# Expert gathers and stores that skip empty places, expert weights loaded early, and two equal halves in the first projection

## The chip, the cores and the metric

The kernel runs on one core of a Trainium2 chip. The metric is the device time of one execution in microseconds (us); lower is better. The kernel before takes 3783.04 us, the median of three runs (3777.04 to 3783.94).

## What is computed

Two transformer blocks over 512 tokens (16 meta tokens stand ahead of them in the first), width 1024, all in float32. The part of the reference that matters here is the first block's mixture of experts, cut to its core:

```python
t = u.reshape(-1, D)                       # 512 tokens x 1024
g_p, g_idx = top_k(softmax(t @ wg + bg), 1)            # one of 8 groups
e_p, e_idx = top_k(softmax(e_logits_of_that_group), 2) # two of its 8 experts
gates = g_p * e_p / sum(e_p)
# every expert e, over the tokens xb that chose it:
hdn = silu(xb @ w_gate[e]) * (xb @ w_up[e])            # 1024 -> 512
ys  = hdn @ w_down[e]                                  # 512 -> 1024
out[token] += gate * ys
```

There are 64 experts, 1024 assignments (two for each token), and three weight matrices of 2 MB for each expert, 403 MB in all. The block's mixer (a gated linear attention and a latent attention behind one input projection of 528 columns) comes first; a second block follows, with a mixer of its own and a feed-forward that gathers single neurons by product keys.

## The kernel before, in words

The program is a row of blocks; at the end of each all engines meet. `setup` loads the activations, kept transposed as `core.h` (128 partitions x 8 x 528), and the first weights. Two weight buffers last through the kernel: `core.w.tiles` (four tiles of 128x8x128, 512 KB each) and `core.w.rows` (2 MB).

`first_mixer` (L672) runs `norm` (L127: squares on ACT, sums by a matmul with ones, the root, the product on DVE), then `project` (L202) of `w_in`: 12 output tiles, for each of them 8 contraction steps. Every step is a matmul of 16 columns (the meta tokens) and one of 512 (the others), `PIECES`; a float32 matmul stands in the trace as two instructions, each with its weight load. ACT copies a finished tile (L695). `by_token` (L277) forms `v` and the low-rank gate input, `gla` and `mla` follow, and `add_projection` (L704) adds `w_out` times their result to `core.h`; it is a `project` over the 512 main columns, whose SP queue fetches tile by tile as PE frees them (L220).

`first_ffn` (L1153) normalises and calls `route` (L711). There SP loads five constants (L749), PE forms the logits of 72 columns (L767) and turns the tokens to rows (L774), which SP writes to `token_rows` (L754). DVE finds the experts, the rank of every assignment within its expert, and its place: expert e owns places 64e to 64e+63, filled from 0 up; what is over 64 goes to spill blocks. POOL scatters the token number of each assignment to its place (L878) in a DRAM table that was cleared to zero, and SP reads the table back as `block_tok` (L758).

`experts` (L885) works through 32 pairs of experts. A pair's 128 places are the 128 partitions. POOL gathers the 128 token rows (L1001), an empty place taking the row of token 0. PE turns them (L919), DVE copies them (L969), and PE runs gate and up (L928) with one expert on each half of the array's columns. ACT applies silu (L956), DVE multiplies (L974), PE turns the hidden values (L937), DVE copies (L979), and PE runs down (L949). ACT copies the result (L962) and stores all 128 rows on its own DMA queue (L964). SP feeds a ring of 8 weight slots of 2 MB, six transfers to a pair, in the order gate, up, down; transfer n waits until the work that used its slot is done (L992). POOL also writes zeros to the 16 spill blocks (L1007). On PE the next pair's tokens are turned between up and the turning of the hidden values, so that ACT's and DVE's work is covered. A second block of the stage would run the spill blocks; no expert has over 64 tokens here, so its loops run nothing.

`combine` (L1108): POOL gathers the two result rows of every token in eight transfers of 128 rows (L1126), DVE weights and adds them (L1137, L1138), PE turns the sums (L1149) and DVE adds them to `core.h`. SP meanwhile loads the next mixer's first tiles and rows (L191, L198).

## Time and profile before

| what | value |
|---|---|
| runs of the kernel before | 3777.04, 3783.04, 3783.94 us |
| the profiled execution | 3787.08 us, span of its instructions 3785.2 us |
| mean granted TensorE clock | 0.87 |
| PE busy, share of the span | 2876.2 us, 76% |
| DVE busy | 1369.1 us, 36% |
| POOL busy | 662.6 us, 18% |
| ACT busy | 552.9 us, 15% |
| DMA | 1047.11 MB, mean 277 GB/s |

The page cuts the span into forty slices of 94.6 us: by them the first mixer takes slices 1 to 5, the router a part of 6 and 7, the experts 7 to 18, the second mixer 18 to 25, and the second feed-forward the rest. The share of busy time is a mean over stages with different limits, so the stages are read apart, by a table of stretches. [...] In a row of the timeline the square brackets hold the idle time before the instruction and what ended it.

### The profile page before, as it was taken

To read this page: it belongs to the slowest core of one execution; us is meant where nothing else is said; L and a number is where in the kernel's file an instruction comes from. 1 tells how busy PE (TensorE), PEld (TensorE's weight loads), DVE (VectorE), ACT (ScalarE), POOL (GpSimd) and SP (SyncE) were. 2 spreads that over 40 slices of the span, in tenths; PEclk is the share of its full clock that TensorE was granted. 3 is DMA by queue.
4 is the path that set the end of the run, shared out by engine and by line. 5 is a ranking of instruction groups with operands and counts; after the bars stand their busy time and mean duration, and the time that the engine had idled before them with its cause. 6 is when DMAs were issued, how large, how long until landed. Compare 5 with 4: busy or idle time off the path is not lost. (4 is left out here: it accounts for less than half of the span.)

```text
span 3785.2 us, 26001 instructions
## 1 busy us (share of the span) xinstructions
PE 2876.2 (76%) x9024; PEld 1313.4 (35%) x9024; DVE 1369.1 (36%) x3223; ACT 552.9 (15%) x1332; POOL 662.6 (18%) x592
## 2 busy tenths in 40 slices
PE   6956884777777777857657989888987787677767
PEld 3432542223333333323254433433443333233223
DVE  1033112000000000012192011566677667766774
ACT  1021100000000000001211010222222222222222
POOL 0000002000000000000120000244343444444433
PEclk9956586899999999978868999999998889888889
DMA  2100005999999999961001212599999999999998
GB/s 96 43 21 0 0 27 234 428 427 427 427 427 427 426 427 427 427 267 34 19 1 61 74 53 78 216 410 398 416 395 400 389 408 406 405 393 412 404 402 333
DMA packets 137673, 1047.11 MB, mean 277 GB/s; under 512 B 20929, under 2 KB 21713, under 8 KB 46929
## 3 DMA queue, kind: packets, MB, share of 16 engines
q0 software_dynamic: 81024, 562.08, 36.5%
q1 hardware_dynamic: 51920, 466.74, 30.1%
q10 hardware_dynamic: 4608, 16.78, 1.1%
q8 instruction: 65, 1.06, 0.1%
q14 instruction: 56, 0.45, 0.0%
HBM read 1020.35 MB, written 25.19 MB: 276 GB/s over the span
## 5 line engine op out<-in xcount | busy, mean ns | idle before, releaser
L1598 PE MATMUL psum<-peer_ring,peer_diag 128*128 128x512 f32 x2048 | 969.6, 632 | 289.9 <-ACT peer_diag L1639 289.6
L1524 POOL DMA_INDIRECT peer_ring<-in_peer_uv,peer_pick x512 | 569.4, 1112 | 1217.6 <-PE psum L1598 747.1
L1731 DVE CUSTOM_DVE_ANT_0 peer_ring<-peer_ring,sb_rows 128x1024 f32<-128x1024 f32 x512 | 618.4, 1224 | 372.6 <-DMA peer_ring<-in_peer_uv,peer_pick 370.8
L1598 PEld LDWEIGHTS psum<-peer_ring,peer_diag 128*128 128x128 f32 x2048 | 408.0, 203 | 843.7 <-issue 483.2
L928 PE MATMUL psum<-moe_w,moe_xT 128*64 128x512 f32 x2048 | 519.0, 664 | 169.3 <-DMA moe_w<-in_w_up 124.3
L974 DVE TENSOR_TENSOR moe_hd<-psum,moe_sg 128x512 f32<-128x512 f32 x32 | 22.1, 692 | 941.3 <-ACT moe_sg L956 941.3
L928 PEld LDWEIGHTS psum<-moe_w,moe_xT 128*64 128x64 f32 x2048 | 181.5, 153 | 505.8 <-issue 504.0
L232 PE MATMUL psum<-mix_xn,sb_tiles 128*128 128x512 f32 x640 | 280.4, 601 | 31.0 <-PEq L1198 20.1
L949 PE MATMUL psum<-moe_w,moe_hT 128*64 128x512 f32 x1024 | 230.0, 601 | 38.4 <-DVE moe_hT L979 33.6
L1001 POOL DMA_INDIRECT sb_tiles<-token_rows,ffn_block_tok x32 | 30.4, 949 | 906.2 <-PE psum L919 905.7
L232 PEld LDWEIGHTS psum<-mix_xn,sb_tiles 128*128 128x128 f32 x640 | 123.5, 193 | 188.0 <-issue 188.0
L1632 ACT ACTIVATE peer_acts<-peer_dots 128x2 f32<-128x2 f32 x256 | 52.0, 203 | 880.4 <-DVE peer_dots L1731 880.4
L1639 ACT ACTIVATE peer_diag<-sb_ident,peer_mix 128x128 f32<-128x128 f32 x512 | 173.5, 386 | 0.4 <-issue 0.2
L949 PEld LDWEIGHTS psum<-moe_w,moe_hT 128*64 128x64 f32 x1024 | 85.3, 138 | 161.1 <-issue 161.1
L1536 PE MATMUL psum<-ffn_hn,sb_tiles 128*128 128x512 f32 x256 | 115.4, 603 | 12.2 <-PEq L139 10.5
L956 ACT ACTIVATE moe_sg<-psum 128x512 f32<-128x512 f32 x32 | 19.1, 598 | 667.7 <-PE psum L928 667.7
L232 PE MATMUL psum<-mix1n_xn,sb_tiles 128*128 128x512 f32 (+1 forms) x384 | 107.1, 436 | 11.3 <-PEq L139 11.3
L878 POOL DMA_INDIRECT slot_tokens<-route_tok,ffn_slots x8 | 8.0, 994 | 597.6 <-DVEq L862 595.5
L962 ACT ACTIVATE sb_tiles<-psum 128x512 f32<-128x512 f32 x64 | 34.7, 595 | 326.9 <-PE psum L949 326.9
L232 PEld LDWEIGHTS psum<-mix1n_xn,sb_tiles 128*128 128x128 f32 x384 | 60.1, 198 | 58.4 <-issue 58.4
L1536 PEld LDWEIGHTS psum<-ffn_hn,sb_tiles 128*128 128x128 f32 x256 | 49.1, 193 | 74.9 <-issue 74.9
L1407 DVE TENSOR_TENSOR mix2b_z<-mix2b_z 128x2048 f32<-128x2048 f32 x1 | 2.3, 2293 | 197.3 <-PEq L214 197.3
(343 smaller groups left out, 2280.0 us busy)
## 6 DMA issues: line engine op xcount, KB each, us to landing
moe_w<-in_w_gate SPq DMA_DIRECT2D x64, 2048.0 KB, 30.2
moe_w<-in_w_up SPq DMA_DIRECT2D x64, 2048.0 KB, 33.2
moe_w<-in_w_down SPq DMA_DIRECT2D x64, 2048.0 KB, 31.0
expert_rows<-sb_tiles ACTq DMA_DIRECT2D x32, 512.0 KB, 10.2
sb_tiles<-in_w_in2b SPq DMA_DIRECT2D x28, 512.0 KB, 3.6
sb_tiles<-in_w_out SPq DMA_DIRECT2D x16, 512.0 KB, 3.5
sb_tiles<-in_w_query SPq DMA_DIRECT2D x16, 512.0 KB, 5.1
peer_ring<-in_peer_uv,peer_pick POOLq DMA_INDIRECT x512
```

Of the source, the lines that this page charges most:

```text
L232: last = nc.tensor.matmul(ps[:, u + 4 * b, 0:c.stop - c.start], wb[:, u, k], rhs[:, k, c], start=k == 0, stop=k == nk - 1)
L928: last = nc.tensor.matmul(ps[r, bank], xT[:, u, k, r], weights(slots[half], k, F, 0, F), start=k == 0, stop=k == KD - 1)
L949: last = nc.tensor.matmul(ps[r, 6 + b], hT[:, k, r], weights(slots[half], k, D, b * 512, 512), start=k == 0, stop=k == KE - 1)
L962: act.activation(yo[:, u, b * 512:(b + 1) * 512], ps[:, 6 + b], ACT.Copy).then_inc(yo_ready, 1)
L974: dve.tensor_tensor(hd[:], ps[:, 3], sg[:], ALU.mult).then_inc(hd_ready, 1)
L1001: pool.indirect_dma_start(out=xg[:, q % 2], out_offset=None, in_=T_rows, in_offset=bass.IndirectOffsetOnAxis(ap=block_tok[:, q:q + 1], axis=0)
L1524: pool.indirect_dma_start(out=ring[:, slot], out_offset=None, in_=A["peer_uv"], in_offset=bass.IndirectOffsetOnAxis(ap=pick[:, i, j:j + 1] ...
L1536: last = nc.tensor.matmul(ps[:, 4 + s], core.w.tiles[:, m % U, k], hn[:, k], start=k == 0, stop=k == KD - 1)
L1598: last = nc.tensor.matmul(ps[:, 2 * i + c], diag[:, b % DIAGS, x], ring[:, slot, D + 512 * c:D + 512 * (c + 1)], start=False, stop=end, sk ...
L1632: act.activation(acts[:, b % DIAGS], dots[:, i, j:j + BATCH], ACT.Gelu).then_inc(gelued, 1)
L1639: act.activation(diag[:, b % DIAGS, x], ident[:], ACT.Copy, scale=mix[:, b % DIAGS, x:x + 1]).then_inc(diagonal, 1)
L1731: dve.tensor_tensor_reduce(ring[:, n % RING, 0:D], ring[:, n % RING, 0:D], hr[:, i], 1.0, 0.0, ALU.mult, ALU.add, dots[:, i, j + x:j + x + ...
```

## The change

- Each place of the table now holds two numbers, the token (for the gather) and the row of the assignment, token + 512j for choice j (for the store). The table is cleared to 2048 instead of 0. Gathers and stores of the experts are both indirect transfers on POOL with a bound (511, 1023), and a place whose number is over it is to be skipped. So results lie in DRAM by assignment; `combine` reads them with four plain transfers of 1 MB on SP ahead of the next mixer's weights. The zero stores of the spill blocks are gone, and DVE clears the two gather buffers at the start.
- The store of a pair moves from ACT's queue to POOL's, behind a wait for both halves of the result; POOL issues gather q+2, then store q.
- The 8 slots of the ring, and the router's constants, are allocated outside the router and filled by SP at the end of the output projection's queue (`then`). To make room, the norm, the router and the experts place their working tiles in `core.w.rows`, `core.w.tiles` and the mixer's `y`. The experts' SP loop starts at transfer 8.
- The first mixer's norm, input projection and low-rank input take their 528 columns as 264 + 264 in place of 16 + 512.

```diff
+HALVES = (slice(0, L // 2), slice(L // 2, L))
...
+MOE_RING = 8
 MOE_BLOCKS = N_EXPERTS + SPILL + 1
+EMPTY = 4 * SEQ
...
-        sq = st.sb("sq", [P, nk, width])
-        mean = st.sb("mean", [P, width])
-        inv = st.sb("inv", [P, width])
-        rs = st.sb("rs", [P, width])
+        if room is None:
+            sq = st.sb("sq", [P, nk, width])
+            mean, inv, rs = (st.sb(n, [P, width]) for n in ("mean", "inv", "rs"))
+        else:
+            sq, (mean, inv, rs) = room
...
+                if then is not None:
+                    then(sp)
...
-            norm(core, "n1", core.h, xn, core.vec[:, VEC["mix"]], D, PIECES)
-            project(core, "in1", A["w_in"], xn, 12, PIECES,
+            norm(core, "n1", core.h, xn, core.vec[:, VEC["mix"]], D, HALVES)
+            project(core, "in1", A["w_in"], xn, 12, HALVES,
                     lambda act, m, acc, c: act.activation(zT[:, m, c], acc, ACT.Copy), following=A["w_out"])
             by_token(core, "in1v", A["w_v"], xn, v,
                      [(i, META + P * i, P) for i in range(NT)] + [(NT, 0, META)],
-                     (A["w_alow"], a_low, PIECES), gla_ahead)
+                     (A["w_alow"], a_low, HALVES), gla_ahead)
...
-                for dst, src in ((wr, "w_router"), (bias, "b_router"), (tri, "before"), (io, "iota"), (tok, "tokens")):
-                    sp.dma_start(dst[:], A[src]).then_inc(loaded, 16)
                 sp.wait_ge(own, 1)
-                sp.dma_start(slot_tok.rearrange("(p n) o -> p (n o)", p=P), zero[:]).then_inc(zeroed, 16)
+                sp.dma_start(slot_tok.rearrange("(p n) o -> p (n o)", p=P), empty[:]).then_inc(zeroed, 16)
...
-                sp.dma_start(block_tok[:], slot_tok.rearrange("(b s) o -> s (b o)", s=2 * SLOTS),
+                sp.dma_start(block_tok[:], slot_tok.rearrange("(b s) o -> s b o", s=2 * SLOTS),
...
-                            in_=tok[:, i:i + 1], in_offset=None).then_inc(scattered[j * NT + i], 16)
+                            in_=tok[:, j, i], in_offset=None).then_inc(scattered[j * NT + i], 16)
...
+        xT = work[:, 0:4].rearrange("p (u a) (k s) -> p u (a k) s", u=2, s=S2)
+        sg, hd = work[:, 4], work[:, 5]
...
-        def result_out(act, row, u, n, wait):
+            act.activation(sg, ps[:, 2], ACT.Silu).then_inc(sg_ready, 1)
+
+        def result_out(act, u, n, wait):
             act.wait_ge(used[DOWN], n + 1)
             act.wait_ge(stored[u], wait)
             for b in range(2):
                 act.activation(yo[:, u, b * 512:(b + 1) * 512], ps[:, 6 + b], ACT.Copy).then_inc(yo_ready, 1)
-            act.wait_ge(yo_ready, 2 * n + 2)
-            act.dma_start(Y_rows[row], yo[:, u]).then_inc(stored[u], 16)
...
-                for n in range(uses):
-                    if n >= RING:
-                        sp.wait_ge(used[(n - RING) % 6 // 2], (n - RING) // 6 + 1)
+                for n in range(RING, uses):
+                    sp.wait_ge(used[(n - RING) % 6 // 2], (n - RING) // 6 + 1)
                     sp.dma_start(wr[:, n % RING], source[n % 6 // 2][2 * (n // 6) + n % 2]).then_inc(landed[n % RING], 16)
 
             @block.gpsimd
             def _(pool):
-                pool.memset(zero[:], 0.0).then_inc(cleared, 1)
+                def take(q):
+                    pool.indirect_dma_start(out=xg[:, q % 2], out_offset=None, in_=T_rows,
+                                            in_offset=bass.IndirectOffsetOnAxis(ap=block_tok[:, q, 0:1], axis=0),
+                                            bounds_check=SEQ - 1, oob_is_err=False).then_inc(gathered[q % 2], 16)
+
+                for q in range(2):
+                    pool.wait_ge(cleared, q + 1)
+                    take(q)
                 for q in range(PAIRS):
-                    if q >= 2:
-                        pool.wait_ge(turned, q - 1)
-                    pool.indirect_dma_start(out=xg[:, q % 2], out_offset=None, in_=T_rows,
-                                            in_offset=bass.IndirectOffsetOnAxis(ap=block_tok[:, q:q + 1], axis=0)
-                                            ).then_inc(gathered[q % 2], 16)
-                    if q == 1:
-                        pool.wait_ge(cleared, 1)
-                        for b in range(N_EXPERTS, MOE_BLOCKS):
-                            pool.dma_start(Y_rows.rearrange("q (b s) d -> (q b) s d", s=SLOTS)[b], zero[:]).then_inc(opened, 16)
-                pool.wait_ge(opened, 16 * (SPILL + 1))
+                    if q + 2 < PAIRS:
+                        pool.wait_ge(turned, q + 1)
+                        take(q + 2)
+                    pool.wait_ge(yo_ready, 2 * q + 2)
+                    pool.indirect_dma_start(out=Y_rows, out_offset=bass.IndirectOffsetOnAxis(ap=block_tok[:, q, 1:2], axis=0),
+                                            in_=yo[:, q % 2], in_offset=None,
+                                            bounds_check=2 * SEQ - 1, oob_is_err=False).then_inc(stored[q % 2], 16)
+                for u in range(2):
+                    pool.wait_ge(stored[u], 16 * (PAIRS // 2))
...
+                    dve.memset(xg[:, u], 0.0).then_inc(cleared, 1)
...
+                placed = Y_rows.rearrange("(j i p) d -> i p j d", j=2, p=P)
+                for i in range(NT):
+                    sp.dma_start(g[:, :, i], placed[i]).then_inc(got[i], 16)
                 first_tiles(core, sp, A["w_in2a"])
                 rows_ahead(core, sp, A["w_v2"])
-
-            @block.gpsimd
-            def _(pool):
-                for i in range(NT):
-                    for j in range(2):
-                        pool.indirect_dma_start(
-                            out=g[:, j, i], out_offset=None, in_=Y_flat,
-                            in_offset=bass.IndirectOffsetOnAxis(ap=slots_u[:, j, i:i + 1], axis=0)
-                        ).then_inc(got[2 * i + j], 16)
 
             @block.vector
             def _(dve):
                 step = Chain(dve, own)
                 for i in range(NT):
-                    dve.wait_ge(got[2 * i], 16)
-                    dve.wait_ge(got[2 * i + 1], 16)
+                    dve.wait_ge(got[i], 16)
...
+                def router_then_experts(sp):
+                    for dst, src in zip(consts, ("w_router", "b_router", "before", "iota", "tokens")):
+                        sp.dma_start(dst[:], A[src]).then_inc(loaded, 16)
+                    source = expert_rows_of(A)
+                    for n in range(MOE_RING):
+                        sp.dma_start(wr[:, n], source[n % 6 // 2][2 * (n // 6) + n % 2]).then_inc(landed[n], 16)
+
+                add_projection(core, "out1", A["w_out"], y, then=router_then_experts)
+                flat = core.w.tiles[:].rearrange("p u k c -> p (u k c)")
+                norm(core, "n2", core.h[:, :, MAIN], y, core.vec[:, VEC["ffn"]], D,
+                     room=(core.w.rows, [flat[:, n * SEQ:(n + 1) * SEQ] for n in range(3)]))
+                route(core, A, y, consts, loaded, T_rows, slot_tok, slots_u, gates, block_tok, spill)
+            experts(core, A, wr, landed, y, T_rows, Y_rows, block_tok, spill)
...
+    places = np.arange(SEQ, dtype=np.uint32).reshape(NT, P).T
+    c["tokens"] = np.stack([np.stack([places, places + j * SEQ], axis=2) for j in range(2)], axis=1)
```

## Rows read from the trace of the kernel before

**Rows 1.** The page, forty slices: DMA busy tenths and GB/s.
```profile
DMA  2100005999999999961001212599999999999998
GB/s 96 43 21 0 0 27 234 428 427 427 427 427 427 426 427 427 427 267 34 19 1 61 74 53 78 216 410 398 416 395 400 389 408 406 405 393 412 404 402 333
```

**Rows 2.** Stretches: length, busy us of each engine (count), PEclk, DMA share, GB/s.
```profile
60.00:148.00 88.00, 86.95 (x321) 48.09 (x320) 0.00 (x0) 7.80 (x22) 0.00 (x0) 1.00 0.18 60
...
500.00:550.00 50.00, 40.33 (x94) 17.39 (x92) 10.50 (x12) 6.18 (x10) 0.00 (x0) 0.94 0.06 21
550.00:600.00 50.00, 24.72 (x124) 23.93 (x124) 23.41 (x99) 5.74 (x11) 2.97 (x3) 0.57 0.14 52
...
640.00:1640.00 1000.00, 779.83 (x3348) 306.70 (x3348) 75.10 (x93) 52.17 (x93) 27.40 (x29) 0.92 1.01 427
...
1645.00:1650.00 5.00, 5.00 (x22) 1.69 (x20) 0.00 (x0) 0.00 (x0) 0.00 (x0) 0.80 0.45 187
```

**Rows 3.** Waits in 610:1662: who waited for whom, us in total, times, longest.
```profile
PE psum L928 <- DMA moe_w<-in_w_up: 124.3, 32, 6.1
```

**Rows 4.** DMA issues: tensor, queue, count, KB each, median us to landing.
```profile
moe_w<-in_w_gate SPq DMA_DIRECT2D x64, 2048.0 KB, 30.2
...
expert_rows<-sb_tiles ACTq DMA_DIRECT2D x32, 512.0 KB, 10.2
...
sb_tiles<-in_w_out SPq DMA_DIRECT2D x16, 512.0 KB, 3.5
...
expert_rows<-moe_zero POOLq DMA_DIRECT2D x16, 256.0 KB, 41.3
...
sb_tiles<-token_rows,ffn_block_tok POOLq DMA_INDIRECT x32, 11.3
```

**Rows 5.** Timeline at the start of the experts: start, us, instruction [idle before it].
```profile
613.08 0.82 SPq L993 DMA_DIRECT2D moe_w<-in_w_gate  x2
...
614.18 0.99 POOL L1001 DMA_INDIRECT sb_tiles<-token_rows,ffn_block_tok  x1 [0.16 <-issue]
...
626.05 1.94 PE L919 MATMUL psum<-sb_ident,sb_tiles 128*128 128x128 f32 x8 [38.04 <-DMA sb_tiles<-token_rows,ffn_block_tok]
628.03 1.23 DVE L969 COPY moe_xT<-psum 128x1024 f32<-128x1024 f32 x1 [26.25 <-PE psum L919]
...
629.32 8.99 PE L928 MATMUL psum<-moe_w,moe_xT 128*64 128x512 f32 x32 [1.32 <-DVE moe_xT L969]
638.35 0.81 SPq L993 DMA_DIRECT2D moe_w<-in_w_up  x2
```

**Rows 6.** Timeline: last w_out tile, start of the route, its first matmul.
```profile
505.76 0.33 SPq L220 DMA_DIRECT2D sb_tiles<-in_w_out  x1
...
552.72 0.09 DVE L801 MEMSET route_zero<- 128x40 uint32 x1 [0.34 <-PEq L139]
...
556.46 13.93 PE L767 MATMUL psum<-route_wr,ffn1r_t 128*128 128x72 f32 x64 [14.29 <-DMA route_tok<-in_tokens]
```

**Rows 7.** Timeline: weight issues released by the ends of up, down, gate.
```profile
1589.87 0.80 SPq L993 DMA_DIRECT2D moe_w<-in_w_down  x2
...
1600.30 0.81 SPq L993 DMA_DIRECT2D moe_w<-in_w_gate  x2
...
1607.17 0.81 SPq L993 DMA_DIRECT2D moe_w<-in_w_up  x2
```

**Rows 8.** Timeline of combine: SP's first issue, PE's first transpose.
```profile
1673.50 1.75 SPq L191 DMA_DIRECT2D sb_tiles<-in_w_in2a  x4
...
1698.27 5.06 PEld L1149 LDWEIGHTS psum<-sb_ident,comb_g 128*128 128x128 f32 x32 [37.43 <-DVE comb_g L1138]
```

**Rows 9.** Timeline: a tile's copy in the first and in the output projection.
```profile
69.20 0.71 ACT L695 ACTIVATE mix_zT<-psum 128x16 f32 x2 [7.94 <-PE psum L232]
...
512.76 0.69 DVE L707 TENSOR_TENSOR sb_h<-sb_h,psum 128x512 f32 x1 [6.18 <-PE psum L232]
```

More of the change, by code:

```diff
@@ L8 @@
+import math
 from contextlib import ExitStack
@@ L124, in sem, with norm @@
         return self.core.sem(f"{self.name}_{name}")
-def norm(core, name, src, dst, gain, dim, pieces=(slice(0, SEQ),)):
+def norm(core, name, src, dst, gain, dim, pieces=(slice(0, SEQ),), room=None):
     nc, ps = core.nc, core.psum
@@ L199, in rows_ahead, with project @@
     core.w.loads += 1
-def project(core, name, w, rhs, n_tiles, pieces, finish, on_vector=False, following=None):
+def project(core, name, w, rhs, n_tiles, pieces, finish, on_vector=False, following=None, then=None):
     nc, ps = core.nc, core.psum
@@ L721, in route @@
     with core.stage("route") as st:
-        wr, bias = st.sb("wr", [P, KD, NR]), st.sb("bias", [P, NR])
-        tri, io, tok = st.sb("tri", [P, P]), st.sb("iota", [P, N_EXPERTS]), st.sb("tok", [P, NT], U32)
-        zero = st.sb("zero", [P, NB * SLOTS // P], U32)
-        rows = st.sb("rows", [P, NT, D])
+        wr, bias, tri, io, tok = consts
+        empty = st.sb("empty", [P, NB * SLOTS // P * 2], U32)
+        rows = core.w.rows[:].rearrange("p (i b) c -> p i (b c)", b=2)
         lg = st.sb("lg", [P, NT, NR])
@@ L800, in _ @@
                 step = Chain(dve, own)
-                step(dve.memset(zero[:], 0))
+                step(dve.memset(empty[:], EMPTY))
                 dve.wait_ge(loaded, 80)
@@ L1024, in _ @@
             def _(dve):
+                for u in range(2):
+                    dve.memset(xg[:, u], 0.0).then_inc(cleared, 1)
                 tokens_out(dve, 0, 0, 0)
@@ L1113, in combine @@
         own = st.sem("own")
-        got = [st.sem(f"got{n}") for n in range(2 * NT)]
+        got = [st.sem(f"got{n}") for n in range(NT)]
         mixed, t_ps, t_out = st.sem("mixed"), st.sem("tps"), st.sem("tout")
@@ L1158, in first_ffn @@
     with core.stage("ffn1") as st:
+        y = st.sb("y", [P, KD, SEQ])
         slots_u, gates = st.sb("slots", [P, 2, NT], U32), st.sb("gates", [P, 2, NT])
-        block_tok, spill = st.sb("block_tok", [2 * SLOTS, MOE_BLOCKS // 2], U32), st.sb("spill", [1, SPILL + 2], U32)
-        with core.stage("ffn1r") as s2:
-            t = s2.sb("t", [P, KD, SEQ])
-            norm(core, "n2", core.h[:, :, MAIN], t, core.vec[:, VEC["ffn"]], D)
-            route(core, A, t, T_rows, slot_tok, slots_u, gates, block_tok, spill)
```

117 lines of the change are left out of this document (62 added, 55 removed).

## The prediction

> **What bounds the kernel now.** I read the page's forty slices first [rows 1]: the DMA engines are full in two stretches only, slices 7 to 16 (the first block's experts) and from slice 26 on (the second block's gathers, which the change leaves alone). The table of stretches says it of the experts [rows 2]: from 640 to 1640 us the DMA share is 1.01 at 427 GB/s while PE is busy 780 of 1000 us. So there a byte costs time and an instruction does not. The waits confirm it: the up projections wait for their weights in all 32 pairs of experts, 124 us in all [rows 3]. Before the experts the DMA engines stand nearly idle: share 0.06 in 500:550 and 0.14 in 550:600 [rows 2]. [...]
>
> **What moves in the expert stage, by bytes.** 192 weight transfers of 2048 KB (2.097 MB) are 402.7 MB; 32 gathers of 128 rows of 4 KB are 16.8 MB, 32 stores of 512 KB 16.8 MB, 16 zero stores of 256 KB 4.2 MB [rows 4]. Up to the last weights (31 stores) that is 439.9 MB, at 427 GB/s 1030 us. The trace has it from the first issue at 613.1 [rows 5] to about 1647 (the share falls to 0.45 in 1645:1650 [rows 2]), 1034 us. I keep the factor 1.004 for the sum after.
>
> **Early ring.** The first 8 weight transfers and the router's 5 constants go to the SP queue behind the last tile of w_out, issued at 505.76 [rows 6]. 17 MB at 427 GB/s take 40 us, so they have landed by some 548, before the route stage begins at 552.7 and before anything else of that queue is due; only the norm computes meanwhile. Without that cover each of the 8 would cost 4.9 us. The constants are there when the router starts: its matmuls now start at 556.46, held by the last constant, and would start about 552.8: -3.7 us [rows 6]. The rest of the route (scatters of 8 bytes in place of 4, the read back of as many short runs, each now 8 bytes) is the same in count; I take 0, between 0 and +2.
>
> At the start of the experts the gather no longer queues behind weights and zeros. Before, it is issued at 614.18 and its rows are turned at 626.05, the first matmul starts at 629.32 and SP issues the next weights at 638.35 [rows 5]. Afterwards, with an empty DMA, I give the gather 3.5 us from issue to turn (a 512 KB tile lands in 3.5 [rows 4]); the memset of its buffer on DVE, which must end first, takes the place of the POOL memset ahead of it now (a copy of 128x1024 takes 1.23 [rows 5], so within 0.3 us). Turn, copy and gate projection keep their 638.35 - 626.05 = 12.3 us. So on the old time base SP issues the ninth load at 614.2 + 3.5 + 12.3 = 630.0, 16.9 us later than the first one now, but with 184 loads left.
>
> **Skipped places.** The reference's own inputs, put through its router, give 1024 assignments, 8 to 31 for each expert, so no spill block, as in the trace, and a quarter of the 4096 places filled. After the ninth load is issued there remain 184 x 2.097 = 385.9 MB of weights, and beside them 30 gathers and 31 stores. What these cost depends on how the 16 DMA engines share the rows, and the view only has their mean. An engine moves 427/16 = 26.7 GB/s, and the weights are ready when the slowest engine is. Places fill from 0 upward in each half of 64, so the filled rows sit on the low partitions of each half. Three ways:
> - Even: a quarter of the rows on each engine, 8.0 MB in all: (385.9 + 8.0)/427 x 1.004 = 926 us.
> - Half: the busiest engine holds four rows that are always filled and four that hardly ever are, where it now carries eight: 385.9/16 + 61 x 4 x 4096 B = 24.12 + 1.00 = 25.12 MB at 26.7, x 1.004 = 945 us.
> - None: an engine holds eight neighbouring places, always filled, or a skipped row moves anyway: (385.9 + 61 x 0.524)/427 x 1.004 = 983 us.
>
> Against 1034 us these give, with the start, 16.9 + 926 - 1034 = -91, -72 and -34 us. I take -72, the middle one: of the two bounds neither is nearer by any row, and the filled places being the low ones speaks against an even split. Of the -72, the early ring is 39 less the 16.9 of the later start, the zero stores 10, and the skipped places the other 40.
> [...]
>
> The stage stays bound by DMA: a pair of experts takes PE, without waits, 6.9 us for the gate (1600.30 to 1607.17, between the issues that its end and that of the work before release), as much for up, and 10.4 from there to the end of down (1589.87 to 1600.30): 24.2 us [rows 7]; DMA needs 945/30.7 = 30.8 (now 32.2). POOL has 2 indirect transfers of about 0.95 us [rows 5] in each 30.8. The store moves from ACT's queue to POOL's. POOL waits there for the pair's result; queued behind it is the gather for three pairs on, which goes out at the end of a pair and no longer after its up projection, 10.4 us later [rows 7]. PE wants it a whole pair and the next one's gate and up later, at least 30.8 + 13.8 = 44.6 us, and it lands in 11.3 [rows 4], so the wait costs nothing; with that slack gone it would cost what the landing is over it. The last store starts one POOL instruction later: +0.7 (0 to 1.5).
>
> **Combine.** Now PE starts at 1698.27, 24.8 us after SP's first issue at 1673.50 [rows 8], behind eight gathers. Afterwards four plain loads of 1 MB go first on SP: 4.2 MB at 427 GB/s are 9.8, plus 2.3 for issue and landing (a 512 KB tile moves in 1.2 and lands in 3.5 [rows 4]), plus DVE's last two passes over 128x1024, 2.4 (a copy takes 1.23 [rows 5]): 14.5. That is -10.3; I take -10 (-6 to -11). The 4 MB for the next mixer move behind them and are due only some 40 us later, after the norm.
>
> **264-column halves.** A tile of the first projection takes 7.94 + 0.71 = 8.65 us from one copy of ACT to the next; the same sixteen 512-column matmuls alone take 6.18 + 0.69 = 6.87 in the output projection [rows 9]. So sixteen 16-column matmuls cost 1.78, 0.111 each, where their columns alone would be 0.013: the weight load that each instruction has must set it. 264 columns take 6.87/16 x 264/512 = 0.221, over 0.111, so the load hides: 32 x 0.221 = 7.08 a tile, 12 x 1.57 = -18.8. The norm has sixteen such pieces more (-1.8), the low-rank extra narrow weights (-0.2). Sum -20.8. Were the load not hidden (0.33 each), it would be +22; the 512-column spacing speaks against that.
>
> **Sum.** -20.8 - 3.7 - 72 + 0.7 - 10 = -105.8. The profiled run is 3787.1 (span 3785.2), 4 over the median of 3783.0; on the median: 3677 us.
>
> **The rivals.**
> - Even split: -91 in place of -72: 3658. For it: nothing in the rows excludes it. Against: the low places.
> - No saving by skipping (or the skip is done in the engines, row by row): -34: 3715.
> - The other side: PE becomes the bound of the experts. With more of its time in work and fewer waits PE could be granted less. At clock c a pair takes 24.2/c. The rest of the change is worth 34 us, so the kernel is slower than before from (1034 - 16.9 + 34)/30.7 = 34.2 us a pair, c under 0.71. At 0.5 a pair takes 48.4 and the kernel 1486 + 16.9 - 1034 - 34 = 435 us longer: 4218. For it: 0.57 over 550:600 [rows 2]. Against: 0.92 in the experts and 1.00 where PE hardly waits [rows 2]. The low level comes after waits here, and these get shorter.
> [...]
> - The change is slight: gathers land over 44.6 us after their issue, behind the stores in POOL's queue, and cost PE the 1.4 us a pair that the bytes give: 3749, between 3740 and 3770. Against: 11.3 us now, with more bytes in flight.
>
> **How the numbers follow.** Chances: half 0.45 (3677, own range 3666 to 3692), even 0.25, none 0.18, slight 0.07, slower 0.05. The range 3648 to 3722 holds the first three but for a few per cent: about 0.83. A measurement of this kernel can tell 0.2% (7.6 us) from no change; faster 0.93, same 0.02, slower 0.05.
>
> **What would show it.** Gathers and stores with a quarter of their packets; on the new time base (24.5 us earlier by the halves and the router) the ninth weights issued near 605; the last weights landed near 1551 (even 1532, none 1589); a rate of 417 GB/s between if the busiest engine sets the pace, 425 if the split is even; router matmuls 0.2 us after the route begins; a tile of the first projection at 7.1 us. A PE without waits in the expert stage, or a granted clock under 0.8, would make the prediction wrong.

## The result, and the profile of the changed kernel

The changed kernel takes 3685.6 us (median of 4 runs, 3680.9 to 3689.3) against 3783.5: a ratio of 0.9735, interval 0.972 to 0.975. Five more runs of it in a later comparison gave 3681.6 us and 0.9725 [0.9708, 0.9742]. I compare the experiments with the middle of the two, 0.973; a thousandth of the ratio is 3.8 us, and a difference of two ratios is known to some 6 to 8 us. The forecast was 3677 us. The profiled run is 3680.9 us with a span of 3678.7, 106.5 less than before.

The page, to be read beside [rows 1]: DMA busy tenths, GB/s, and the packets with how many of them are short.

```profile
DMA  2100055999999999721002222999999999999998
GB/s 108 56 0 0 1 211 193 426 426 426 426 425 416 423 414 412 326 94 45 9 24 74 71 60 69 372 404 410 395 394 399 405 405 410 396 409 400 407 388 337
...
DMA packets 136328, 1017.83 MB, mean 277 GB/s; under 512 B 26752, under 2 KB 27536, under 8 KB 45584
```

Three things are to be seen. Slice 6 now carries 211 GB/s: the early ring, in a stretch that stood empty. The experts' stretch ends almost a slice earlier. And inside it the rate is no longer the flat 427 of [rows 1]: it starts at 426 and sags to 412 to 423, while the busy digit stays 9. The stretches say it more exactly (length, busy us of each engine with its count, PEclk, DMA share, GB/s; beside [rows 2]). PEclk is the clock granted to TensorE as a share of its full one, DMA share the mean busy share of the 16 DMA engines, up to 1.01 here:

```profile
620.00:1000.00 380.00, 312.26 (x1389) 127.04 (x1386) 30.03 (x38) 21.87 (x39) 26.56 (x26) 0.96 1.01 426
1000.00:1300.00 300.00, 239.78 (x1046) 94.40 (x1048) 23.20 (x29) 16.23 (x29) 20.44 (x20) 0.93 1.01 421
1300.00:1500.00 200.00, 159.28 (x703) 63.79 (x701) 16.94 (x21) 10.69 (x19) 12.26 (x12) 0.95 1.00 414
...
1540.00:1550.00 10.00, 6.70 (x25) 2.29 (x23) 0.00 (x0) 0.00 (x0) 0.00 (x0) 0.83 0.39 162
```

The share falls to 0.39 over 1540:1550, centred near 1544, but that is the mean of the engines. In the trace's records each weight transfer has 16 landings, as many as there are DMA engines; those of the last weights come between 1537.1 and 1555.6, where before they came between 1644.7 and 1651.4. The waits of PE for weights are 97.5 us where they were 124.3 [rows 3], with the gate's beside them; the stage is still bound by DMA, and the granted clock is 0.93 to 0.96.

```profile
PE psum L938 <- DMA ffn1w_w<-in_w_up: 97.5, 29, 4.5
PE psum L938 <- DMA ffn1w_w<-in_w_gate: 34.4, 26, 2.7
```

The timeline from the last tile of w_out to the ninth weights, the lines that answer to [rows 5] and [rows 6]:

```profile
486.25 0.33 SPq L225 DMA_DIRECT2D sb_tiles<-in_w_out  x1
486.78 0.33 SPq L1184 DMA_DIRECT2D ffn1r_wr<-in_w_router  x1
...
489.05 0.91 SPq L1187 DMA_DIRECT2D ffn1w_w<-in_w_gate  x2
...
533.16 2.17 PE L775 MATMUL psum<-ffn1r_wr,ffn_y 128*128 128x72 f32 x9 [10.50 <-PEq L144]
533.21 0.12 DVE L809 MEMSET route_empty<- 128x80 uint32 x1 [0.35 <-PEq L144]
...
591.40 1.04 POOL L1005 DMA_INDIRECT sb_tiles<-token_rows,ffn_block_tok  x1 [8.23 <-DVE sb_tiles L1039]
...
594.92 1.94 PE L929 MATMUL psum<-sb_ident,sb_tiles 128*128 128x128 f32 x8 [30.25 <-DMA sb_tiles<-token_rows,ffn_block_tok]
...
598.18 15.42 PE L938 MATMUL psum<-ffn1w_w,ffn_y 128*64 128x512 f32 x64 [1.31 <-DVE ffn_y L977]
606.78 0.82 SPq L1000 DMA_DIRECT2D ffn1w_w<-in_w_up  x2
```

The gather's rows are turned 3.5 us after its issue, where it took 11.9; gate and up of the first pair run as one group of 64 matmuls with no wait for weights between them; SP issues the ninth weights at 606.78. From the issue of the last tile of w_out to the start of the route it is 533.21 - 486.25 = 46.96 us, and before, by [rows 6], 552.72 - 505.76 = 46.96 too: the early weights cost the norm beside them nothing.

And the end of the stage, beside [rows 8]: the last copy of a result on ACT, its store on POOL, the combine's loads and its first transposes.

```profile
1565.02 1.08 ACT L972 ACTIVATE sb_tiles<-psum 128x512 f32<-128x512 f32 x2 [9.69 <-PE psum L959]
...
1566.88 0.97 POOL L1017 DMA_INDIRECT expert_rows<-sb_tiles,ffn_block_tok  x1 [28.86 <-ACT sb_tiles L972]
...
1582.83 2.22 SPq L1139 DMA_DIRECT2D comb_g<-expert_rows  x4
...
1597.53 5.53 PE L1160 MATMUL psum<-sb_ident,comb_g 128*128 128x128 f32 x32 [32.55 <-DVE comb_g L1149]
```

Between POOL's store and SP's loads lie 15.95 us in which no engine computes. The copy on ACT came 11.7 us ahead of the combine's first issue before; now it is 17.8. What fills them is in the view of the block's own line:

```profile
L995 POOLq COMPARE_BRANCH  x1: 42/42/42, 1569.6 to 1569.6; - x1
L995 POOLq DRAIN  x1: 5274/5274/5274, 1569.7 to 1569.7; - x1
L995 SPq EVENT_SEMAPHORE  x1: 17/17/17, 1575.2 to 1575.2; - x1
```

POOL's store has landed by 1569.6, POOL's end of the block takes 5.27 us from there, the other engines are let go at 1575.2, and the empty loops of the spill block take the rest, to 1582.8. In the kernel before, POOL came to its end at 1558, a hundred microseconds early, and its 12.9 us cost nothing:

```profile
L987 POOLq DRAIN  x1: 12944/12944/12944, 1558.1 to 1558.1; - x1
```

ACT's last copy of a result in the kernel before, which the sum needs too:

```profile
1661.76 1.08 ACT L962 ACTIVATE sb_tiles<-psum 128x512 f32<-128x512 f32 x2 [9.70 <-PE psum L949]
```

**The sum, measured at the combine's first transpose** (before minus after, from the rows): to the start of the route 552.72 to 533.21, -19.5; router 3.74 to -0.05, -3.8; from there to ACT's last copy, 1661.76 to 1565.02 less the first two, -73.4; the tail +6.1; the combine 24.77 to 14.70, -10.1. Together -100.7, which is also what the medians say (97.9 us in the first comparison, 104.4 in the second). The other 5.8 us of the spans come after 1600, in code that is the same in both.

### The profile page after: what moved, and what is told of

It reads as the page before. It is cut to its first block and busy times, and to the rows that moved or that the text cites. A ratio compares the mean times of both kernels' runs of the same rounds, so it can differ in the third digit from the quotient of the medians.

```text
span 3678.7 us, 26039 instructions
## 1 busy us (share of the span) xinstructions
PE 2829.1 (77%) x9024; PEld 1327.2 (36%) x9024; DVE 1370.8 (37%) x3225; ACT 552.5 (15%) x1332; POOL 680.0 (18%) x599
## 5 line engine op out<-in xcount | busy, mean ns | idle before, releaser
L938 PE MATMUL psum<-ffn1w_w,ffn_y 128*64 128x512 f32 x2048 | 501.8, 647 | 133.2 <-DMA ffn1w_w<-in_w_up 97.5
L982 DVE TENSOR_TENSOR ffn_y<-psum,ffn_y 128x512 f32<-128x512 f32 x32 | 22.1, 692 | 882.2 <-ACT ffn_y L966 882.2
L938 PEld LDWEIGHTS psum<-ffn1w_w,ffn_y 128*64 128x64 f32 x2048 | 180.9, 148 | 452.7 <-issue 450.9
L959 PE MATMUL psum<-ffn1w_w,moe_hT 128*64 128x512 f32 x1024 | 226.8, 594 | 36.1 <-DVE moe_hT L987 33.7
L1017 POOL DMA_INDIRECT expert_rows<-sb_tiles,ffn_block_tok x32 | 32.6, 1018 | 898.1 <-ACT sb_tiles L972 898.1
L959 PEld LDWEIGHTS psum<-ffn1w_w,moe_hT 128*64 128x64 f32 x1024 | 84.5, 137 | 156.3 <-issue 156.3
L886 POOL DMA_INDIRECT slot_tokens<-ffn1r_tok,ffn_slots x8 | 8.0, 996 | 574.3 <-DVEq L870 572.1
L966 ACT ACTIVATE ffn_y<-psum 128x512 f32<-128x512 f32 x32 | 19.1, 597 | 606.6 <-PE psum L938 606.6
L239 PE MATMUL psum<-mix1n_xn,sb_tiles 128*128 128x264 f32 x384 | 87.4, 392 | 11.3 <-PEq L144 11.3
L239 PEld LDWEIGHTS psum<-mix1n_xn,sb_tiles 128*128 128x128 f32 x384 | 74.1, 193 | 24.6 <-issue 11.7
```

The lines of the kernel that those rows point to most:

```text
L239: last = nc.tensor.matmul(ps[:, u + 4 * b, 0:c.stop - c.start], wb[:, u, k], rhs[:, k, c], start=k == 0, stop=k == nk - 1)
L938: last = nc.tensor.matmul(ps[r, bank], xT[:, u, k, r], weights(slots[half], k, F, 0, F), start=k == 0, stop=k == KD - 1)
L959: last = nc.tensor.matmul(ps[r, 6 + b], hT[:, k, r], weights(slots[half], k, D, b * 512, 512), start=k == 0, stop=k == KE - 1)
```

## Experiments

One number stands for a kernel's stream of expert weights below: the time from SP's issue of the ninth weights to POOL's last store. In the changed kernel it is 606.78 to 1566.88, 960.1 us, and in three experiments that leave the stream as it is (the pieces, and the two on the tail) 961.0, 961.0 and 961.3, so it repeats to about a microsecond, much better than whole runs do. It has two parts: until PE starts the last up projection, which waits for its weights in every one of the profiles, and PE's own work from there to the store. The first part is 939.1 us in the changed kernel and 937.5 to 940.2 in the profiles of the kernels that leave the stream as it is; the second is 19 to 24 us and depends on the clock that PE is granted just there, as the last experiment shows (23.6 us where it was 0.50, 19.3 where it was 1.00). A trace is one execution, so its differences need not be those of the medians.

### The places of a half spread over its partitions

```
 step(dve.tensor_copy(slots_u[:], slf[:]))
+step(dve.tensor_scalar(whole[:], slots_u[:], 8128, None, ALU.bitwise_and))
+step(dve.tensor_scalar(part[:], slots_u[:], 4, None, ALU.logical_shift_right))
+step(dve.tensor_scalar(part[:], part[:], 3, None, ALU.bitwise_and))
+step(dve.tensor_tensor(whole[:], whole[:], part[:], ALU.add))
+step(dve.tensor_scalar(part[:], slots_u[:], 15, None, ALU.bitwise_and))
+step(dve.tensor_scalar(part[:], part[:], 2, None, ALU.logical_shift_left))
+step(dve.tensor_tensor(whole[:], whole[:], part[:], ALU.add))
+step(dve.tensor_copy(slots_u[:], whole[:]))
```

> Edit: the places of a half are permuted so that ranks 0 to 15 of an expert sit four partitions apart. Theory A (the DMA engines share a transfer by fixed partitions and the one that holds the always filled low places sets the pace): the busiest engine goes from 4 filled rows a transfer to 2, 2 x 2 x 0.16 = 0.64 us less a pair, so -19.7 us in the expert stage, +1.6 for eight more small DVE steps in the router: 18 below the changed kernel, ratio to before about 0.969. The 16 completions of a weight load land within 3 us of each other at the end of the stage (19 in the changed kernel). Theory B (the rows are shared evenly already and the stage is slower than 427 GB/s for another reason): no change but the +1.6, ratio 0.974.

3667.4 us, ratio 0.9684 [0.9667, 0.97]: 17 us under the changed kernel. The ninth weights go out at 610.4, 3.6 us later: 1.1 is there when the route starts, 2.5 are the eight added steps. The stream takes 945.1 us, 15.0 less (until the last up projection 921.5, 17.7 less); the rate no longer sags:

```profile
620.00:1000.00 380.00, 313.16 (x1420) 127.69 (x1422) 31.76 (x40) 21.87 (x39) 26.56 (x26) 0.97 1.01 426
1000.00:1300.00 300.00, 240.46 (x1066) 96.24 (x1062) 24.04 (x30) 16.82 (x30) 20.42 (x20) 0.95 1.01 426
1300.00:1500.00 200.00, 161.61 (x712) 64.00 (x712) 14.69 (x19) 11.18 (x20) 13.27 (x13) 0.95 1.01 426
```

Of the two ratios expected it is the smaller. The same bytes move; only which partition a row goes to differs. So the split of the rows over the DMA engines was on the path. The expectation added up 19.7 less and 1.6 more; the trace has 15.0 (17.7) less and 2.5 more. The last store comes 11.4 us earlier in the trace, less than the 17 of the ratio: the profiled execution was the slowest of the four, 3675.2 us.

### The filled places packed on as few partition groups as possible

Small steps on DVE as in the run above, with these terms:

```
+whole = place & 8128
+whole += place & 3
+whole += (place & 4) << 3
+whole += (place >> 1) & 28
```

> Edit: the places of a half are permuted so that ranks 0 to 7 sit on partitions 0 to 3 and 32 to 35 of the half. Theory A: the busiest engine carries 8 filled rows in each gather and store in place of 4, 2 x 4 x 0.16 = 1.28 us more a pair: +39 us in the stage, ratio about 0.984, with as few bytes moved as in the changed kernel. Theory B: nothing but +1.6 in the router, ratio 0.974.

3730.0 us, ratio 0.9856 [0.984, 0.9873]: 48 us over the changed kernel, near the 0.984 of the theory of uneven engines and far from the other. The stream takes 1002.3 us, 42.2 more (40.9 until the last up projection), again with the same bytes:

```profile
620.00:1000.00 380.00, 306.57 (x1344) 122.85 (x1346) 29.44 (x37) 21.28 (x38) 26.62 (x26) 0.94 1.00 417
1000.00:1300.00 300.00, 228.41 (x990) 89.88 (x986) 21.78 (x27) 15.14 (x27) 18.43 (x18) 0.93 0.98 397
1300.00:1500.00 200.00, 157.20 (x662) 61.68 (x664) 14.52 (x18) 10.10 (x18) 12.29 (x12) 0.91 0.98 398
```

398 GB/s at a share of 0.98: the mean share hardly tells that one engine holds up the others, the rate does.

### Every place moves a row

Here nothing is skipped: an empty place gathers token 0 and stores its result to a row of its own that nobody reads.

```
-sp.dma_start(slot_tok..., empty[:])
+sp.dma_start(slot_tok..., A["empties"])      # token 0; row 2 * SEQ + place
-bounds_check=2 * SEQ - 1
+bounds_check=2 * SEQ + MOE_BLOCKS * SLOTS - 1
```

> Edit: no place is skipped: an empty place gathers token 0 and stores to a row of its own that nobody reads. Theory A: every engine then carries 8 rows in each transfer, the busiest 4 more than now: +39 us, the same as with the packed places though 24 MB more move. Theory B (even now): 24 MB at 427 GB/s, +57 us. A skipped place that costs a short packet only is common to both; if skipping were free of gain (rows moved anyway): +0.

3721.8 us, ratio 0.9829 [0.9812, 0.9845]: 37.5 us over the changed kernel. The stream takes 993.3 us, 33.2 more (34.9 until the last up projection), for 25 MB more, at the full rate of the kernel before:

```profile
620.00:1000.00 380.00, 306.45 (x1336) 122.00 (x1338) 29.10 (x37) 21.27 (x38) 25.49 (x25) 0.93 1.01 427
1000.00:1300.00 300.00, 237.07 (x1012) 92.93 (x1010) 21.78 (x27) 15.14 (x27) 19.45 (x20) 0.92 1.01 427
1300.00:1500.00 200.00, 157.04 (x682) 62.65 (x680) 16.94 (x21) 10.69 (x19) 12.25 (x12) 0.93 1.01 428
```

25 MB at 427 GB/s are 59 us: that is what skipping would have given with an even split, and it gave 33 to 37. That is near the 39 of the expectation for uneven engines and far from the 57 for even ones.

**The three together.** In the raw records a 16 KB packet of weights takes 0.61 us on its engine, a 4 KB row 0.159 and a skipped place leaves a packet of 4 bytes and 0.009 us. Which partitions each of the 16 engines serves no run shows one by one, but the landings below count filled rows. In the changed kernel the last engine falls behind the first by 8.4 rows a pair. In the packed kernel, which puts the eight places of a half that are always filled on its partitions 0 to 3 and 32 to 35, it is 15.6 (1.1 to 17.6 us from round 2 to round 7, 6.7 pairs), so these eight go to one engine, gathered and stored. I read that as four and as eight rows in each gather and each store: over the 32 pairs the busiest engine has 128 filled rows in the changed kernel and 256 in the packed one. When all move, 4096 rows over 16 engines are 256 each, and the mean of the 1024 filled ones is 64. For the spread kernel, whose split was not counted, the table takes that mean as the lowest that its busiest engine can have. A row is gathered and stored, 0.318 us:

| kernel | rows of the busiest engine | worked out | stream measured | difference | difference until the last up projection |
|---|---|---|---|---|---|
| spread | 64 or more | -20.4 at most | 945.1 | -15.0 | -17.7 |
| changed | 128 | 0 | 960.1 | 0 | 0 |
| packed | 256 | +40.7 | 1002.3 | +42.2 | +40.9 |
| all rows | 256 | +40.7 | 993.3 | +33.2 | +34.9 |

So packed fits to 2 us. The 15.0 to 17.7 us of spread are 47 to 56 rows at 0.318, by which its busiest engine would still have 72 to 81. (Net of the two short packets that a skipped place leaves, a row is worth 0.300 us, and the worked out column becomes -19.2 and +38.4; the fit of packed is then one of 4 us.) All rows, with the busiest engine as full as in the packed kernel, is 6 to 9 us better than it: with uneven engines something is lost beyond the busiest one's bytes (the mean 16 KB packet takes 0.634 us in the packed kernel, 0.621 in the changed one, 0.615 in the other two). What, stays open.

The records show the mechanism at work too. The time from the first of a weight transfer's 16 landings to the last, for the weights of one slot of the ring, round by round (us):

```
before    1.4  2.2  1.8  2.7  2.7  2.2  2.2  2.5  3.2  3.3  4.2  3.7  ...  6.6
changed   1.4  1.1  2.5  4.7  5.8  9.3 10.4 11.5 14.0 15.2 16.3 18.8  ... 19.4
spread    1.9  1.2  2.0  2.2  2.6  3.0  3.5  3.8  4.3  4.4  4.6  5.2  ... 11.5
packed    1.5  1.1  3.9  8.1 10.5 15.2 17.6 19.9 21.2 21.5 22.4 22.9  ... 20.0
all rows  1.0  1.1  2.0  1.9  2.1  2.5  2.2  2.4  2.7  3.5  3.6  4.6  ...  7.3
```

The rates fit: 426 GB/s while the distance still grows, 414 to 421 after, and sooner and lower in the packed kernel. The spread kernel ends at 11.5 us where its expectation had 3, and the kernel before at 6.6: the spread split is not quite even.

### The ring issued late again

```
 def router_then_experts(sp):
     ...
-    for n in range(MOE_RING):
-        sp.dma_start(wr[:, n], ...)
...
-for n in range(RING, uses):
-    sp.wait_ge(used[...], ...)
+for n in range(uses):
+    if n >= RING:
+        sp.wait_ge(used[...], ...)
```

> The first eight weight transfers of the experts are issued in the experts' block again, as before, rather than behind w_out in the first mixer's last block; nothing else differs. If the early ring is worth what the account says, the ninth transfer stops being free at the start: the DMA engines stand idle from the end of w_out to the experts' block, and 8 transfers of 2.1 MB, some 39 us at 420 GB/s, move behind it. Of the 39 us the 16.8 us in which the changed kernel's ninth transfer waits for a slot anyway (first issue of the block possible at about 590, ninth weights at 606.8) come off, so +22 us: ratio 0.980. Rival: the ring was hidden anyway, or only its first pair counts (10 us): ratio 0.976. Rival on the other side: the first gather of tokens stands behind the eight transfers again, as in the kernel before, and costs its 12 us more (not on the path, if the stream of weights is what bounds): ratio 0.983.

3710.0 us, ratio 0.9785 [0.9769, 0.98]: 21 us over the changed kernel, as worked out. In the trace the last store is at 1592.97, 26.1 later, 1.7 of it already there when the route starts. The rival on the other side is half right: the gather does queue behind the weights, turned 10.7 us after its issue in place of 3.5, and PE starts that much later, but the stream had its eight transfers to move meanwhile, so it is not on the path.

```profile
593.12 1.04 POOL L1006 DMA_INDIRECT sb_tiles<-token_rows,ffn_block_tok  x1 [8.26 <-DVE sb_tiles L1040]
...
603.81 1.94 PE L929 MATMUL psum<-sb_ident,sb_tiles 128*128 128x128 f32 x8 [37.45 <-DMA sb_tiles<-token_rows,ffn_block_tok]
...
615.66 0.80 SPq L1001 DMA_DIRECT2D ffn1w_w<-in_w_up  x2
```

The stretch that the early ring fills, in this kernel and then in the changed one: share 0.00 against 1.00.

```profile
500.00:530.00 30.00, 22.50 (x52) 9.42 (x50) 6.94 (x7) 6.18 (x10) 0.00 (x0) 0.97 0.00 0
```

```profile
500.00:530.00 30.00, 20.82 (x48) 8.66 (x46) 8.64 (x9) 6.18 (x10) 0.00 (x0) 0.93 1.00 429
```

PE's busy time a 512-column matmul, 0.43 us, is the same in both, so the ring costs the projection and the norm beside it nothing that shows.

### The pieces of 16 and 512 columns again

```
-norm(core, "n1", ..., D, HALVES)
-project(core, "in1", A["w_in"], xn, 12, HALVES, ...)
+norm(core, "n1", ..., D, PIECES)
+project(core, "in1", A["w_in"], xn, 12, PIECES, ...)
```

> Edit: the first mixer's 528 columns again as 16 + 512, the rest of the change kept. Theory: each 16-column matmul costs its weight load, 0.11 us, and 264 columns hide it: +19 to +22 us (12 tiles x 1.6 and the norm's 1.8), ratio about 0.979. Rival (264 columns don't hide their load either, the gain in the first stage came from the clock): under +10.

3704.6 us, ratio 0.9785 [0.9769, 0.9801]: 21 us over the changed kernel, in the range expected and out of the rival's (under 10). A tile's two copies, here and then in the changed kernel:

```profile
78.62 0.71 ACT L701 ACTIVATE mix_zT<-psum 128x16 f32 x2 [7.94 <-PE psum L239]
```

```profile
75.59 0.67 ACT L701 ACTIVATE mix_zT<-psum 128x264 f32 x2 [6.45 <-PE psum L239]
```

8.65 us a tile against 7.12. The load of the mask, issued when the first projections are done, stands at 149.35 and 150.12 us in the two kernels with pieces and at 127.66, 128.66, 129.13 and 129.69 in four with halves: 20.9 us between the means, and a scatter of 2 us from one execution to the next.

### The tail: the combine in the experts' block

Here the spill blocks are left out (on this input none of them runs), and the combine's loads, sums and transposes stand in the experts' block behind waits of their own, its loads in the ring's slots 0 and 1.

```
 with nc.Block() as block:            # the experts
     @block.sync
     ...
+        for u in range(2):
+            sp.wait_ge(stored[u], 16 * (PAIRS // 2))
+        for i in range(NT):
+            sp.dma_start(g[:, :, i], placed[i]).then_inc(got[i], 16)
...
-with nc.Block() as block:            # the spill blocks
-with nc.Block() as block:            # the combine
```

> The two spill blocks that may follow the experts are left out (no expert of this input has more than 32 assignments, so they compute nothing), and the combine's loads, sums and transposes stand in the experts' block, each behind a wait of its own. Only POOL then stands at the end of its block, beside the combine's work. If POOL's end of block (5.3 us in the records behind its last store) and the empty spill loops (7.6 us) are on the path, both go: 13 us less than the changed kernel, ratio 0.970. If the end of block only moves (the combine's own end waits for it), 8 us less: 0.9715. If neither is on the path, no change: 0.974.

3669.9 us, ratio 0.9681 [0.9667, 0.9694]: 18.5 us under the changed kernel, of which the trace accounts for 13:

```profile
1568.42 0.97 POOL L1029 DMA_INDIRECT expert_rows<-sb_tiles,ffn_block_tok  x1 [27.55 <-ACT sb_tiles L977]
1571.12 1.99 SPq L1010 DMA_DIRECT2D ffn1w_w<-expert_rows  x4
...
1585.81 6.61 PE L1050 MATMUL psum<-sb_ident,ffn1w_w 128*128 128x128 f32 x32 [19.28 <-DVE ffn1w_w L1067]
```

2.70 us from store to load in place of 15.95, -13.25, and 17.4 from store to the first transpose in place of 30.65. POOL's end of block is still 5.27 us long, from 1571.3, but now it lies beside the loads.

### The tail: the spill block left out alone

Only the second block of the experts is left out. It was run in two comparisons.

> The spill block is left out and nothing else is moved (it computes nothing on this input): POOL's end of block stays on the path and the 7.6 us of the empty loops go. Expected 7.6 us less than the changed kernel, ratio 0.972; the gap from ACT's last copy of a result to the combine's first load falls from 17.8 to about 10 us. If the loops ran under POOL's end of block instead, nothing: 0.974.

> The kernel without the spill block (it computes nothing on this input) once more: by the gap from POOL's last store to the combine's first load, 15.95 us against 8.38, it should be 7.6 us under the changed kernel of the same call; against runs of another call it came out 11 to 16 under. If something besides the gap is saved, the difference stays over 11.

> The changed kernel itself, beside two of the experiments on one chip at one time, since the kernel before took 3783 to 3789 us from one call to the next and the gains in question are 8 to 31 us. Expected ratio 0.973 to 0.974.

First 3674.3 us, ratio 0.9692 [0.9679, 0.9706], which is 14 us under the changed kernel, about twice what was expected. Beside the changed kernel itself on one chip: 3672.3 us (ratio 0.9703 [0.9684, 0.9723]) against 3681.6, 9.3 us; by the two intervals such a difference is known to some 10 us, so here the trace decides. From POOL's last store to the combine's loads it is 8.38 us:

```profile
1570.55 0.97 POOL L1017 DMA_INDIRECT expert_rows<-sb_tiles,ffn_block_tok  x1 [33.09 <-ACT sb_tiles L972]
1578.93 2.24 SPq L1071 DMA_DIRECT2D comb_g<-expert_rows  x4
```

15.95 - 8.38 = 7.57, as expected to the tenth: the loops stood behind POOL's end of block and not under it. The 14 us of the first comparison stand against changed kernels of other comparisons; 9.3 and 7.57 agree within what runs can tell. So the 15.95 us are 2.7 (issue and landing of the store), 5.3 and 0.4 (POOL's end and the block's), 7.6 (loops).

### Both together

The spread places, and the combine in the experts' block with the spill loops kept, ahead of its loads. Nothing of the computation is left out. Run in two comparisons.

```
+slots_u = (place & 8128) + ((place >> 4) & 3) + ((place & 15) << 2)
...
     @block.sync
     ...
+        spilled(sp, body)
+        for u in range(2):
+            sp.wait_ge(stored[u], 16 * (PAIRS // 2))
+        ... # loads of the combine
```

> The places of a half are spread over its partitions (as in the run that spread them) and the combine stands in the experts' block, with the spill loops kept ahead of its loads. The two gains lie in different stretches and should add: 18 us from the spread stream and, since the loops are kept, 5 to 8 us from POOL's end of block, which now lies beside the combine. Expected 24 us less than the changed kernel, ratio 0.967; if the loops also overlap, 31 us, 0.965; if the spread stream leaves POOL's last store later against the last weights, only 18: 0.969.

> The kernel with spread places and the combine in the experts' block once more: by the traces 15 us of the stream, less 3.6 of the added route steps, and 13.4 of the tail: 25 us under the changed kernel of the same call, give or take 4.

3658.0 us, ratio 0.9652 [0.9639, 0.9666], and 3652.9 us, 0.9648 [0.9631, 0.9665], beside 3681.6 for the changed kernel on one chip: 28.7 us less. The larger of the gains expected of the tail came true, 13 us: SP runs through its empty loops while the last pair still computes, so they overlap although they are kept.

```profile
1554.31 0.97 POOL L1057 DMA_INDIRECT expert_rows<-sb_tiles,ffn_block_tok  x1 [32.87 <-ACT sb_tiles L987]
1556.83 2.04 SPq L1038 DMA_DIRECT2D ffn1w_w<-expert_rows  x4
...
1571.73 6.52 PE L1104 MATMUL psum<-sb_ident,ffn1w_w 128*128 128x128 f32 x32 [19.32 <-DVE ffn1w_w L1126]
```

The stream takes 945.0 us, the step from store to loads 2.52, the first transpose comes 25.8 us earlier than in the changed kernel: -15.1 +2.6 (the later ninth weights, 609.4) -13.2.

In the second comparison the same program's stream takes 940.8 us, 4.2 less, and its first transpose comes 28.2 us earlier than in the changed kernel beside it, which is what the medians say. The last up projection starts in both at 921.4 and 921.5 us behind the ninth weights; what differs is PE's work behind it. In the first profile and then in the second:

```profile
1530.73 9.97 PE L953 MATMUL psum<-ffn1w_w,ffn_y 128*64 128x512 f32 x32 [3.03 <-DMA ffn1w_w<-in_w_up]
```

```profile
1530.58 7.09 PE L953 MATMUL psum<-ffn1w_w,ffn_y 128*64 128x512 f32 x32 [3.00 <-DMA ffn1w_w<-in_w_up]
```

The granted clock over 1530:1535 is 0.50 in the first and 1.00 in the second, after the same wait of 3 us in both; the first rises to 0.84 over 1535:1540. The run that only spread the places fell on the first side (10.03 us, 0.60 over 1530:1535). So of what spreading gives the stream, 17.7 us repeat in three profiles, and the clock of the last pair makes 15 or 19 of them.

## Why the prediction was right, and where it missed

- **What bounds the stage: right.** DMA share 1.01 to 1.00, waits for weights in 29 pairs, granted clock 0.93 to 0.96 (0.92 before). The rival of PE as the bound found nothing: the level did not fall under 0.9 in any of the three stretches.
- **Early ring: right.** Its place held, the ninth weights went out at 606.8 for "near 605", the gather took 3.5 us for 3.5. The later start of the stream is 17.0 us on the old base (606.78 against 613.08 less 23.3), for 16.9. Issued late again it costs 21 us by the medians and 24 by the trace, for the 22 of 39 - 16.9.
- **Skipped places, the case "half": right, and shown.** From the ninth weights to ACT's last copy 958.2 us; 945 and the last pair's 14.8 (1661.76 less 1647) were 959.8. "Last weights landed near 1551" needs care: the fall of the mean share, from which the 1647 of the kernel before was read, now comes near 1544, because most engines are done early. By the last of the 16 landings it is 948.8 us from the ninth weights, for 945 and the 4.4 by which 1647 was early (1651.4). No row of the kernel before shows the four rows of its busiest engine, on which the 945 of the forecast stands; in their place the landings show the 8.4 rows a pair, four gathered and four stored. The rivals "even" and "none" differ from it only in how the engines share the rows, and the spread and packed kernels moved just that, by -15 and +42 us of stream with the same bytes. "None" fell with them: with every row moved the kernel is 37 us slower. Its own number for the even split, 19 us less, was not quite reached by spreading (15, or 17.7 until the last up projection); the spread split is not even, by the 15.0 to 17.7 us some 72 to 81 rows on the busiest engine against a mean of 64. The estimate of 417 GB/s for the stretch fits the later part (421 and 414) and not the first 380 us (426); the prediction had not thought of the light engines running ahead. Of the -72 it gave the skipping 40, the ring 22 and the zero stores 10. The experiments give 33 to 37 for the skipping and 21 to 24 for the ring; by the traces that leaves 16 of the 73.4 for the zero stores and all else, and no run takes the zero stores apart.
- **The choice between the cases** rested on the low places being the filled ones and on a middle of two bounds, since no row of the kernel before could tell them apart. It held, but a chance of 0.45 was what such an argument is worth.
- **Halves: right.** -20.8 was said, -20.9 is the distance of the means; 7.12 us a tile for 7.08. In the one profiled pair 19.5 of it was left at the route. That the 0.111 us of a 16-column matmul are its weight load was inferred and is not shown; the runs show the time of a tile, 8.65 us against 7.12.
- **Router: right**, -3.8 for -3.7; its matmuls start 0.05 us before DVE's first instruction of the route, for "0.2 us after it begins".
- **The last store on POOL: the term that was mis-sized.** "+0.7 (0 to 1.5)" counted one more instruction in the chain. It measured +6.1. The one more instruction is there, 0.75 us (1.86 from ACT's copy to POOL's store, where ACT issued its own 1.11 behind the copy), and the other 5.3 are POOL's end of the block. The step that failed is the bound: it came from the length of instructions, and took the end of a block to be free. With the store, POOL became the last engine of the block, and brought with it an end of block that had lain 100 us ahead of the others'. Its row stood in the trace of before, 12.9 us of it, in a view of the block's line that the prediction did not ask for; nor had it asked what the 11.7 us between ACT's last copy and the combine were made of, 7.6 of them empty loops.
- **Combine: right**, -10.1 for -10.
- **The sum.** -105.8 was said and -100.7 measured at the same point; the tail's 5.4 us are the difference, while the halves (+1.3) and the stage (-1.4) cancel, and with them the forecast of 3677 would have been 3682, between the two medians of the changed kernel.
- **A rival's number.** "The change is slight" was put at 3749, but its 1.4 us a pair over 30.7 pairs are 43 us, and 3677 + 43 = 3720: it left out what the early ring saves. It plays no part in the forecast, and after the first gather PE waits for none.

## What to carry to other kernels

When a gather or store skips places, ask what the busiest DMA engine saves and not what the mean saves (here 33 to 37 us by the first, where the bytes left out are 59 us at 427 GB/s), and try the filled places spread over the partitions (here 15 to 19 us of stream for eight steps on small tiles, 2.5 us). When work moves to another engine at the end of a block, ask which engine now ends the block last and what its end costs, and put what follows into the same block behind its own wait where it can go (13 us here, with the empty loops). To compare small gains read the traces between two fixed events, which repeat to one to three microseconds, end at the event that waits for the resource in question and not behind it, and compare medians of kernels that ran together.

## What the runs showed of the hardware that was not expected

- A skipped place is not nothing here: it leaves a packet of 4 bytes that takes 0.009 us; the page counts 5823 more packets under 512 B than before. POOL's gather takes 1.02 us on average with the bound and 0.95 without.
- POOL's end of the experts' block takes 5.27 us, the same in all twelve profiles of kernels that store from POOL, and 12.9 us in the kernel before, which also had plain transfers of zeros on that queue. What it does in that time, and whether the zeros made it longer, the records don't say.
- The mean DMA share stays at 0.98 to 1.01 while the rate falls from 427 to 397 GB/s: that one engine is behind in its work could not be told from the share. The time between the first and the last of the 16 landings of one transfer told it at once: 6.6 and 7.3 us at the end of the two even streams, 11.5 with the spread places, about 20 in the two uneven ones.
- The same matmuls of the last pair ran at a granted clock of 0.50 at first in one execution of a program and at 1.00 in another, 9.97 us against 7.09, after the same wait of 3 us.
